# Transposes one unit and value products two units behind the scores in the single-head softmax stage

## What is computed

```python
def block(qblk):                       # first block, grouped-query heads
    sc = jnp.einsum('bgrqd,bgkd->bgrqk', qblk, kt).astype(jnp.float32)
    p = jax.nn.softmax(sc, axis=-1).astype(vt.dtype)
    return jnp.einsum('bgrqk,bgkd->bgrqd', p, vt)
...
logits = jnp.einsum('bqhd,bqkhd->bqhk', qb, ksel).astype(jnp.float32) * (A_HEAD_DIM ** -0.5)
logits = logits + bias.astype(jnp.float32)           # second block, selected keys
logits = jnp.where((rel >= 0)[:, :, None, :], logits, -jnp.inf)
p = jax.nn.softmax(logits, axis=-1).astype(v.dtype)
return jnp.einsum('bqhk,bqkhd->bqhd', p, vsel)
```

## Time and profile before

| | |
|---|---|
| median of three runs | 3418.18 us (3412.99 to 3421.04) |
| the profiled execution | 3412.95 us |
| its span in the trace | 3411.2 us, so 1.75 us lie outside the span |
| mean granted TensorE clock over the span | 0.796 of full speed |
| plain stage, layer 1 of the first block | about 341 to 481 us from the start of the span |
| plain stage, layer 2 of the first block | about 880 to 1021 us |
| masked stage | about 1738 to 1888 us |

### The profile page before, as it was taken

One profiled execution on the slowest core, in us unless ns is written; L12 is line 12 of the kernel. 1 busy time (PEld: TensorE's weight loads), 2 busy tenths in 40 slices (PEclk: granted clock), 3 DMA queues, 4 the chain that ended last, 5 costly groups with the idle time before them and its releaser, 6 DMA issues. The chain is left out here.

```text
span 3411.2 us, 45824 instructions
## 1 busy us (share of the span) xinstructions
PE 2788.7 (82%) x18417; PEld 2577.8 (76%) x18417; DVE 1237.9 (36%) x2097; ACT 1033.5 (30%) x1535; POOL 499.4 (15%) x369
## 2 busy tenths in 40 slices
PE   5984978895697796669658989999896777799998
PEld 4973758894577696569447989999895554799998
DVE  1236232325423323331642344342323444343442
ACT  3233332225232210221323243231214444232232
POOL 0002100001100101200123033030002222032130
PEclk6996557897557698779555799999896666899998
DMA  3210001220001121011000223332220000232321
GB/s 105 87 50 6 1 3 50 87 75 6 1 1 52 38 75 42 19 50 56 33 1 0 68 75 84 97 91 77 71 79 1 0 0 0 62 83 77 105 74 59
DMA packets 232723, 165.44 MB, mean 48 GB/s; under 512 B 7439, under 2 KB 229513, under 8 KB 232421
## 3 DMA queue, kind: packets, MB, share of 16 engines
q1 hardware_dynamic: 232548, 162.91, 16.0%
HBM read 160.76 MB, written 2.14 MB: 48 GB/s over the span
## 5 line engine op out<-in xcount | busy, mean ns | idle before, releaser
L252 DVE TENSOR_TENSOR panel_lo<-panel_raw,panel_hi 128x2048 fp32r<-128x2048 f32 (+2 forms) x155 | 335.1, 2162 | 361.6 <-ACT panel_hi L244 361.6
L244 ACT ACTIVATE panel_hi<-panel_raw 128x2048 fp32r<-128x2048 f32 (+2 forms) x155 | 276.4, 1783 | 597.1 <-PE product L319 464.7
L328 PE MATMUL product<-panel_hi,normed_hi 128*128 128x256 f32 (+1 forms) x1336 | 378.7, 283 | 10.2 <-PEq L541 10.2
L328 PE MATMUL product<-panel_hi,normed_lo 128*128 128x256 f32 (+1 forms) x1336 | 378.6, 283 | 0.0
L328 PE MATMUL product<-panel_lo,normed_hi 128*128 128x256 f32 (+1 forms) x1336 | 378.6, 283 | 0.0
L319 PE MATMUL product<-scaled_hi,panel_hi 128*128 128x264 f32 x1408 | 289.9, 287 | 19.6 <-DVE scaled_lo L2097 12.5
L319 PE MATMUL product<-scaled_lo,panel_hi 128*128 128x264 f32 x1408 | 289.7, 287 | 0.0
L319 PE MATMUL product<-scaled_hi,panel_lo 128*128 128x264 f32 x1408 | 289.5, 287 | 0.0
L328 PEld LDWEIGHTS product<-panel_hi,normed_hi 128*128 128x128 f32 x1336 | 258.1, 193 | 10.2 <-issue 10.2
L328 PEld LDWEIGHTS product<-panel_hi,normed_lo 128*128 128x128 f32 x1336 | 258.2, 193 | 0.0
L328 PEld LDWEIGHTS product<-panel_lo,normed_hi 128*128 128x128 f32 x1336 | 258.1, 193 | 0.0
(11 more groups left out here) (278 smaller groups left out, 5508.2 us busy)
## 6 DMA issues: line engine op xcount, KB each, us to landing
panel_raw<-in_w_in_dram SPq DMA_DIRECT2D x26, 1024.0 KB, 5.3
panel_raw<-in_ffn_w_gate_dram SPq DMA_DIRECT2D x44, 512.0 KB, 4.0
panel_raw<-in_ffn_w_up_dram SPq DMA_DIRECT2D x44, 512.0 KB, 5.3
panel_raw<-in_ffn_w_down_dram SPq DMA_DIRECT2D x32, 704.0 KB, 4.6
panel_raw<-in_even_w_in_dram SPq DMA_DIRECT2D x21, 1024.0 KB, 5.2
panel_raw<-in_odd_w_in_dram SPq DMA_DIRECT2D x12, 1024.0 KB, 5.1
panel_raw<-in_w_out_dram SPq DMA_DIRECT2D x8, 1024.0 KB, 5.1
panel_raw<-in_even_w_out_dram SPq DMA_DIRECT2D x8, 768.0 KB, 4.8
```

The lines of the kernel that those rows point to most:

```text
L244: act.activation(c.hi[g % 2][:, 0:used], c.raw[g % 2][:, 0:used], ACT.Copy).then_inc(c.hi_made.sem, 1)
L252: dve.tensor_tensor(c.lo[g % 2][:, 0:used], c.raw[g % 2][:, 0:used], c.hi[g % 2][:, 0:used].bitcast(F32), ALU.subtract).then_inc(c.lo_made ...
L328: done = pe.matmul(out[:, 0, 0:v - u], a[:, k, t * P:(t + 1) * P], w[:, k, u:v], start=(k == 0 and x == 0), stop=(k == chunks - 1 and x == 2))
```

## The change

The two distances become variables. For kind "diff" they stay 2 and 3. For kind "heads" they become 1 and 2: turn n of TensorE's loop holds S(n), T(n-1), M(n-2), the copies on ScalarE and the divisions on VectorE follow in the same way, and the loops have U+2 turns instead of U+3. No instruction is added or removed, no buffer changes its size, and every wait counts to the same unit as before.

```diff
@@ softmax_stage
     U, M = len(units), len(units) * per_unit
     e_ring = 4
+    turn_after, mix_after = (2, 3) if diff else (1, 2)
@@ scalar
-                    for n in range(U + 3):
+                    for n in range(U + mix_after):
                         if n == 1:
                             stage_high(i, 1)
                         if n < U:
                             exponentials(i, n)
-                        if 2 <= n <= U + 1:
-                            copy_turned(i, n - 2)
-                        if n >= 3 and diff:
-                            copy_mixed(i, n - 3)
+                        if turn_after <= n < U + turn_after:
+                            copy_turned(i, n - turn_after)
+                        if n >= mix_after and diff:
+                            copy_mixed(i, n - mix_after)
@@ tensor
-                    for n in range(U + 3):
+                    for n in range(U + mix_after):
                         if n < U:
                             score(i, n)
-                        if 2 <= n <= U + 1:
-                            turn(i, n - 2)
-                        if n >= 3:
-                            mix(i, n - 3)
+                        if turn_after <= n < U + turn_after:
+                            turn(i, n - turn_after)
+                        if n >= mix_after:
+                            mix(i, n - mix_after)
@@ vector
-                    for n in range(U + 3):
+                    for n in range(U + mix_after):
                         if n < U:
                             logit(i, n)
...
                             if 1 <= n <= U:
                                 invert(i, n - 1)
-                            if n >= 3:
-                                divide(i, n - 3)
+                            if n >= mix_after:
+                                divide(i, n - mix_after)
```

## The result

Over seven runs each, the changed kernel has a median of 3424.93 us (3420.48 to 3428.52) and the kernel before 3413.91 us (3412.94 to 3421.04). The ratio is 1.0026, with a 95% interval of 1.0014 to 1.0038: slower by some 9 us, between 5 and 13. The forecast was +7.4 us, slower by just over 0.2%. The profiled execution took 3424.93 us with a span of 3423.1 us, 11.9 more than before.

The account below looks back on a forecast made before the run. TensorE, busy throughout the loops at the lower clock, was taken as the bound. Four plain bodies at 1.77 us (+7.1) and the masked stage (+0.3) gave +7.4 us on 3418.2, so 3425.6 us, range 3415 to 3433.

Parts of the forecast that it names:

- The bound: Middle of plain and masked bodies: TensorE busy throughout, 50.00 of 50.00 and 45.00 of 45.00 us, at clock 0.50.
- Part 1, the start: Start of a plain body: hole before T(0) grows from 0.39 to 1.65 us, S(2) paid in line, one score group behind.
- Part 2, the body: Loop and drain of a plain body: one full turn less one score-free pair, 1.77 us later, +7.1 us for four.
- Part 3, no new wait in the loop: Steady plain turn: shorter distances leave 2.7 us for T, 2.8 for M, no cost; masked stage 0.1 us per body.
- Part 4, the masked stage: Masked bodies: 0.13 us gained at the start, 0.20 and 0.1 lost, about +0.15 per body, +0.3 us for two.
- the wait of 0.74 us: Start of a masked body: T(1) waits for the copy of unit 0; this wait was to be gone.
- The level: Whole kernel: +7.4 us on the median of three runs before, 3418.2, giving 3425.6 us.
- The clock opens in the drains: Last body of all three stages: a clock rise gains up to 2.15 us each, 6.5 in all, no change; chance 0.08.
- A new wait in the loop: Loop: T waits for the exponential each turn, say 0.2 us, adding 21 us: 3446; short masked units +8: 3434; chance 0.05.
- the drain is what counts: Drain: each of six bodies loses one score-free turn of 2.45 us, 14.7 us faster, 3403.5; chance 0.02.
- not on the path: Start of a plain body: the hole doesn't count or S(2) passes the waiting T(0), nothing changes, 3418.5; chance 0.04.
- The clock rises in the loops: Plain loops at full clock: turn of 2.11 us, chain of 3.09 us the nearer limit, 59 us less, some 3366; chance 0.02.

Follow-up runs that it names:

- score2_early: The changed kernel with S(2) put in front of T(0) again in the plain stages; ratio to the kernel before 1.0009 (0.9997 to 1.0020).
- turn_only: Only the transposes move up in the plain stages, T(n-1) and M(n-3) in turn n, masked stage as before; ratio to the kernel before 1.0024.
- deeper: Distances 3 and 4 in the plain stages, 2 and 3 elsewhere; ratio to the kernel before 0.9981 (0.9969 to 0.9992).
- pairs_12: Changed kernel with S(n+1) right behind S(n) for even n in the plain stages, distances 1 and 2 there; ratio to the kernel before 0.9721.
- score_pairs: Distances 2 and 3 as before, S(n+1) right behind S(n) for even n in the plain stages; ratio to the kernel before 0.9701, median 3340.52 us.

## Why the prediction was right, point by point

- **The bound.** TensorE without a hole in the loop at the lower clock: unchanged in the after profile.
- **Part 1, the start.** Expected a hole of 1.65 us in front of T(0), measured 1.66; T(0) at 3.31 us; one score group behind at the same distance from the start. score2_early and turn_only show it to be the cause: the first puts S(2) back into the hole and 1.04 of the 1.78 us go, the second moves only T and its copy and 1.65 of them come.
- **Part 2, the body.** +1.77 expected, +1.78 measured in both layers; 7.1 for four bodies, and 3.56 + 3.56 measured.
- **Part 3, no new wait in the loop.** The plain turn is 4.22 us, and TensorE busy 50.00 of 50.00; in the middle of the masked body it is 45.00 of 45.00. Held.
- **Part 4, the masked stage.** +0.3 expected, +0.20 and +0.15 in the two profiles. The single times came out to 0.01 us. Wrong was the sentence that the wait of 0.74 us would be gone: it was read as a hole of its own, but is the remainder of one late bias, and it now stands as 3.9 us on the same row. A wait of T(0) for its exponential, 1.31 us, is new there and was not foreseen; it takes the place of the 0.71 in front of S(2). The sum was made from times, not from these rows, and so wasn't touched.
- **The level.** The sum of +7.4 was set on a median of three runs, 3418.18; over seven the median of before is 3413.91. That the forecast of 3425.6 came within 1 us of 3424.93 is luck: the level of before was 4.3 us too high, and the two medians lie 11.0 us apart, 3.6 more than the +7.4, which the softmax stages (7.3 and 7.1 us in two profiles) don't show. The ratio is the fairer test: +9 us with 5 to 13, where +7.4 was said. It is compatible with the forecast and too wide to confirm its size; the lengths of the stages do that.
- **The rivals.** *The clock opens in the drains* happened: one drain of the first plain stage rose to 0.82, and one of the second. But these were the drains between two bodies, where a rise gains nothing. The drain that ends the masked stage stayed cold in its profile, as in that of before. The mechanism is real all the same: in deeper, score2_early and turn_only the last 20 loads of the masked stage took 2.91 to 2.96 us instead of 4.96, and the stage was some 2 us shorter, close to the 2.15 I had put on it. What I called once in six bodies is common: that drain was warm in four of the eleven profiles (these three and pairs_12), so the masked stage differs by 2 us for a reason that isn't the edit's. *A new wait in the loop*, *the drain is what counts* and *not on the path* are excluded by the rows above. *The clock rises in the loops* didn't occur here; it did with pairs. Why the clock rises in one drain and not in another, no run shows.

## What to carry to other kernels

When the engine that bounds a loop is busy throughout, moving consumers nearer to producers has no wait in the loop to remove, and it can take away the work that stood in front of the first wait of the body. Count the list of work done at one fixed distance from the start in both orders. Here the difference, priced at one turn less one score-free turn, was the cost of a body; with pairs it all but vanished (+0.26 us), so the start has to be counted again for each order. And look at the start itself for things that run better there than in the loop: here it showed two score groups running at once, which was worth about 44 us by the order alone, six times the 7 us of the distances, and more with the clock.

## What the runs showed of the hardware that I had not expected

- Score groups of 64 rows on different halves run together in the loop as well as at the start: two groups took the place of one in each turn, 6.69 us for two units against 8.44. The Trainium skill, TensorE: Matmul & The Clock Gate, section "Part 3: Packing small matmuls — row/col tiling", says that matmuls on different row tiles of the array run at the same time; the trace agrees for two halves of 64 rows, also inside a loop, where the two groups stand next to each other.
- With the same matmuls packed so, the clock rose in most bodies. Before, a stage with TensorE busy 130.93 of 135 us stayed at 0.50. With pairs in all single-head stages it was busy 73.39 of 84 us, and the mean clock was 0.82. In deeper only S(0) to S(3) are packed, and the clock rose right behind them in all four bodies, for some 4 us. But the second body of score_pairs, in layer 1, is packed throughout and stayed at 0.50. Busy time alone, then, doesn't tell the level, and neither does packing. What the clock goes by wasn't tried here. The rule cited with the prediction, that a busy engine gets 2.4 GHz, doesn't hold for the plain stages of before.
- One and the same program had its retention stage at a mean clock of 0.70 in one profile and 0.82 in another, 5 us apart. A difference in one profile outside the edited stages needs a second profile before it is given a cause.
